# One decoder layer step on one core: decode softmax steps one key group later, small loads on three queues, a weight split forward

## The chip, the cores and the metric

The kernel runs on one core of one Trainium2 chip. The metric is the device time of one execution in microseconds (us). The kernel before takes 1120.18 us (median of three runs, 1119.37 to 1123.1).

## The reference

One step of a hybrid layer over 512 prompt tokens and 8 single decode tokens, all in float32. After an adaptive RMS norm a projection `w_in` feeds two groups of heads: a gated linear recurrence (RG-LRU) and latent attention (MLA). Cut to what matters here:

```python
mod = silu(c) @ w_ada + b_ada                      # shift, scale and gate of both halves
z = (rms_norm(x, norm1_g) * (1 + scale1) + shift1) @ w_in
x_lru, g_lru, q_lat, kv_lat, k_rope = split(z)
lru_out = rg_lru(causal_dwconv(x_lru)) * gelu(g_lru)
q = rms_norm(q_lat, q_lora_norm_g) @ w_uq;  kv_lat = rms_norm(kv_lat, kv_lora_norm_g)
# decode, for each of 8 sequences: 4096 cached keys (paged) and the new one, 8 heads
lat = concat(cache_lat[pages], lat_new)            # 4097 x 128
kv = lat @ w_ukv;  k_nope = rms_norm(kv[..., :64], k_nope_g);  v = kv[..., 64:]
p = softmax((q_nope . k_nope + q_rope . kr) * 96 ** -0.5);  attn = p @ v
x = x + gate1 * (concat(norm(lru_out), norm(attn)) @ w_o)
x = x + gate2 * gated_conv_mlp(...)                # w_up, w_down: the largest products
```

## The kernel before

Every engine has a program of its own, written by hand in the order in which it runs; semaphores join them. TensorE (PE) uses four PSUM tiles `ps0` to `ps3` in a fixed rotation: each piece of work has a job number j and takes `ps[j % 4]`, so PE may start job j only when job j - 4 has been read out by ScalarE (ACT) or VectorE (DVE) (`claim`).

**Start.** SyncE (SP) issues the inputs and the 24 chunks of `w_ada` of 1 MB into a ring of four slots; chunks 4 and on wait until PE has used the slot (`chunk_used`). ACT first issues 25 small loads (parameter rows, decode states, the page table), then a tanh (L1329) which the first product needs. PE turns x (eight jobs), does chunks 0 and 1, turns the parameter rows, does chunks 2 and 3.

**Input projection.** Twelve column tiles of `w_in`, `w0` to `w11`, are each split by ACT into a high part (`in_high`) and by GpSimd (POOL) into a low part (`in_low`), and PE multiplies them (`w_in(n)`, 48 matmuls each). `IN_ORDER` is the order of PE's jobs. ACT's `gate_branch(k)` reads out the gate tiles: `gate_branch(0)` frees the PSUM tile of `w8`. `nq`, `nkv`, `kr0` are sums of squares for three norms; ACT's `rstd` turns each into a reciprocal root.

**Decode.** Each of the 8 sequences is a unit v of 33 key tiles in nine groups g (eight of four tiles, one of one). PE runs two groups ahead with transposes: at group g it turns the latents of group g + 2 (at g = 7 and 8 those of groups 0 and 1 of the next unit), then multiplies group g (L1174). ACT copies the turned latents (L1512) and their high part (L1513), POOL takes the low part (`low_latents`, L795), and PE's group g waits for that. ACT squares the keys (L1528), DVE sums them (L2009).
The softmax of unit v - 1 lies within unit v: DVE `scores_max` in group 1 (L1964 to L1971), POOL `all_max` at g = 2 (L779, a maximum over all partitions), DVE `shift` in group 2 (L1976), ACT `probs` (L1506), DVE `prob_sums` (L1981), and PE `pv` (L1130, L1134) after group `PV_AT` = 4. When `pv` is done, the latents of unit v - 1 may be overwritten, and POOL fetches those of unit v + 1 into their place with two indirect DMAs of 1 MB (`cached_latents`, L749); the first half is needed by the transposes of group 0 of the next unit, at g = 7. POOL runs all this in one fixed order. In POOL's program the compiler puts an instruction MODIFY_POOL_CONFIG ahead of the maximum (before its wait), and another behind it.

Of the kernel before, what the change touches and what calls it, by code (L numbers as in the profile page):

```python
# [32 lines left out]
P = 128  # L33
# [78 lines left out]
class Steps:  # L112
# [20 lines left out]
    def leave(self, laps):  # L133
# [18 lines left out]
            + ["w6", "r4", "w7", "c3", "w8", "w9", "nq", "nkv", "kr0", "r5", "w10", "c4", "w11", "kr1", "c5"])  # L152
# [55 lines left out]
PV_AT = 4  # L208
# [49 lines left out]
def build(nc, t):  # L258
    with ExitStack() as ctx:
# [308 lines left out]
        def _(sp):  # L568
# [148 lines left out]
        def _(pool):  # L717
            nc.gpsimd.memset(par_rows[:, :, :], 0.0).then_inc(s_parz, 1)
            nc.gpsimd.memset(BD[:, :, :, :], 0.0).then_inc(s_bdz, 1)

# [78 lines left out]
            for v in range(1, NS + 1):  # L799
                for g in range(NG):  # L800
# [31 lines left out]
        def _(pe):  # L832
# [135 lines left out]
            w_in(9)  # L968
# [8 lines left out]
            both(j, C("blk", QK, R)[:, NOPE:QK], sq[NOPE:QK, 3, :], True, True, R).then_inc(psum_full[j % 4], 1)  # L977
            later_chunk(12)
# [309 lines left out]
        def _(act):  # L1288
# [19 lines left out]
            for name in ("b_ada", "norm1_g", "lru_conv_b", "lru_b_a", "lru_b_x", "lru_lambda",  # L1308
                         "q_lora_norm_g", "kv_lora_norm_g", "lru_out_norm_g", "mla_out_norm_g", "norm2_g"):
                load_rows(name, t[name].rearrange("l (r p) -> (l r) p", p=P))  # L1310

            load_rows("lru_conv_w", t["lru_conv_w"].rearrange("l w (r p) -> (l w r) p", p=P))
            for name, a, b in (("gq", "q_nope_norm_g", "q_rope_norm_g"), ("gk", "k_nope_norm_g", "k_rope_norm_g")):
                r = ROWS[name]
                act.dma_start(par_rows[r:r + 1, 0, 0:NOPE], t[a]).then_inc(s_par, 16)
                act.dma_start(par_rows[r:r + 1, 0, NOPE:QK], t[b]).then_inc(s_par, 16)
            fw = t["ffn_conv_w"].rearrange("l w (r p) -> (l w r) p", p=P)
            act.dma_start(par_rows[0:4 * FT, 1, :], fw[0:4 * FT, :]).then_inc(s_par, 16)
            act.dma_start(par_rows[0:2 * FT, 2, :], fw[4 * FT:6 * FT, :]).then_inc(s_par, 16)
            act.dma_start(par_rows[2 * FT:4 * FT, 2, :],  # L1320
                         t["ffn_conv_b"].rearrange("l (r p) -> (l r) p", p=P)).then_inc(s_par, 16)
            act.dma_start(st_tok, t["state_lru_conv"].rearrange("l b r w -> (l b r) w")).then_inc(s_par, 16)
            act.dma_start(h0_tok, t["state_lru_h"].rearrange("l b w -> (l b) w")).then_inc(s_par, 16)

            for r in range(4):
                act.dma_start(page_of[r:P:4, :], t["page_table"].rearrange("b n -> n b"), allow_slow_non_contiguous=True).then_inc(s_pt, 16)
# [55 lines left out]
            in_high(9)  # L1382

# [131 lines left out]
            def unit(base, lap, e, v):  # L1515

                for g in range(NG):
# [13 lines left out]
                    if base != J_DEC and g == 2:  # L1531
# [675 lines left out]
```

## Time and profile before

| | |
|---|---|
| median of three runs | 1120.18 us |
| profiled execution | 1124.76 us |
| its span (first to last instruction) | 1123.0 us |
| busy: PE, DVE, ACT, POOL | 1005.5, 671.2, 537.9, 196.8 us |
| mean granted clock of PE | 0.937 of 2.4 GHz |

The page lists engines' busy time; the views used below are the waits (which engine stood still for whom), the timelines (instructions in order of time, with the idle time before each), the chain of work that ended last, and tables by stretch of time. Decode lies between 308 and 645 us.

### The profile page before, as it was taken

Reading aid. Unit: us, or ns where it says so; the run is one execution under the profiler, and the core shown is the slowest. Engines: PE = TensorE matmul, PEld = TensorE weight load, DVE = VectorE, ACT = ScalarE, POOL = GpSimd, SP = SyncE. Lnnn points to the kernel's source line nnn. Section 1 sums busy time; section 2 is a strip of 40 time slices with the busy share of each in tenths; the row PEclk is TensorE's granted clock in tenths of the full one; section 3 lists DMA queues with packets and bytes.
Section 4 is the critical chain, followed back from the end, with each engine's and each line's share of the span. In section 5 each row is a group of like instructions: output and inputs, shape, how many; then the busy total and the mean of one; then the engine's idle time right before and its main releaser. Section 6 shows DMA issues by size and latency. Waiting matters only on the chain.

```text
span 1123.0 us, 21332 instructions
## 1 busy us (share of the span) xinstructions
PE 1005.5 (90%) x7916; PEld 904.9 (81%) x7916; DVE 671.2 (60%) x1553; ACT 537.9 (48%) x875; POOL 196.8 (18%) x202
## 2 busy tenths in 40 slices
PE   6699989999797977978978699799999999999997
PEld 4388755444496977977878689699999999999997
DVE  4591356656676657567557545667777777753212
ACT  3314736555487758658658443344444434322210
POOL 0233231000123422432432202211000010100000
PEclk9699987988899999899899879899999999999999
DMA  8975534000100211211201014222423233263202
GB/s 292 303 244 180 187 117 156 13 10 2 49 18 20 95 50 45 93 34 60 92 21 56 1 38 132 51 76 75 112 75 110 77 94 93 81 177 91 71 3 77
DMA packets 110527, 100.28 MB, mean 89 GB/s; under 512 B 10451, under 2 KB 99454, under 8 KB 108381
## 3 DMA queue, kind: packets, MB, share of 16 engines
q1 hardware_dynamic: 105478, 78.36, 23.5%
q0 software_dynamic: 3456, 20.97, 5.3%
q8 instruction: 36, 0.59, 0.2%
q10 hardware_dynamic: 1539, 0.22, 0.1%
q14 instruction: 18, 0.15, 0.0%
HBM read 96.80 MB, written 2.94 MB: 89 GB/s over the span
## 4 chain that ended last, share of the span: by engine, by line
PE 70%; DVE 9%; ACT 8%; issue 8%; POOL 2%; DMA 1%; ACTq 1%; DVEq 0%; POOLq 0%; SPq 0%
PE ps L841 46%; PE ps L1174 12%; PE ps L836 4%; PE ps L1078 2%; PE ps L866 2%; POOL latents_low L795 2%; DMA RW<-w_ada 1%; PE ps L1134 1%; DVE RB L2009 1%; ACT RB L1528 1%; DVE RB L1893 1%; ACT RB L1512 1%; PE ps L1169 1%; PE ps L1042 1%; PE ps L1059 1%
## 5 line engine op out<-in xcount | busy, mean ns | idle before, releaser
L841 PE MATMUL ps<-normed_high,up_weights_high 128*128 128x260 f32 x704 | 142.7, 284 | 3.6 <-DVE normed_low L1728 3.4
L841 PE MATMUL ps<-normed_high,up_weights_low 128*128 128x260 f32 x704 | 142.3, 284 | 0.0
L841 PE MATMUL ps<-normed_low,up_weights_high 128*128 128x260 f32 x704 | 142.1, 284 | 0.0
L795 POOL TENSOR_TENSOR latents_low<-RB,latents_high 128x512 fp32r<-128x512 f32 (+1 forms) x72 | 86.1, 1202 | 274.6 <-ACT latents_high L1513 224.6
L1174 PE MATMUL ps<-key_weights_high,latents_high 128*128 128x260 f32 x528 | 120.7, 312 | 13.0 <-DVE RB L2007 11.8
L841 PEld LDWEIGHTS ps<-normed_high,up_weights_high 128*128 128x128 f32 x704 | 109.2, 190 | 4.3 <-issue 3.5
L1174 PE MATMUL ps<-key_weights_low,latents_high 128*128 128x260 f32 x528 | 111.4, 294 | 0.0
L1575 ACT ACTIVATE up_weights_high<-RW 128x1024 fp32r<-128x1024 f32 x44 | 46.6, 1060 | 135.4 <-PE ps L841 132.9
L1174 PE MATMUL ps<-key_weights_high,latents_low 128*128 128x260 f32 x528 | 111.3, 294 | 0.0
L841 PEld LDWEIGHTS ps<-normed_high,up_weights_low 128*128 128x128 f32 x704 | 109.0, 189 | 0.0
L841 PEld LDWEIGHTS ps<-normed_low,up_weights_high 128*128 128x128 f32 x704 | 108.8, 189 | 0.0
L1174 PEld LDWEIGHTS ps<-key_weights_high,latents_high 128*128 128x128 f32 x528 | 87.2, 204 | 16.7 <-DVE RB L2007 14.7
L1174 PEld LDWEIGHTS ps<-key_weights_high,latents_low 128*128 128x128 f32 x528 | 86.8, 201 | 0.0
L1174 PEld LDWEIGHTS ps<-key_weights_low,latents_high 128*128 128x128 f32 x528 | 86.8, 201 | 0.0
L2088 DVE TENSOR_TENSOR up_weights_low<-RW,up_weights_high 128x1024 fp32r<-128x1024 f32 x44 | 54.9, 1251 | 34.3 <-ACT up_weights_high L1575 29.9
L1528 ACT ACTIVATE qrot<-ps 128x512 f32<-128x512 f32 x88 | 52.9, 601 | 45.4 <-PE ps L1174 41.7
L841 PE MATMUL ps<-hidden_high,down_weights_high 128*128 128x260 f32 x352 | 71.4, 284 | 1.3 <-issue 1.3
L2006 DVE COPY RB<-ps 128x32 f32<-128x32 f32 (+1 forms) x72 | 13.6, 188 | 96.1 <-ACT qrot L1528 52.4
L841 PE MATMUL ps<-hidden_high,down_weights_low 128*128 128x260 f32 x352 | 70.8, 282 | 0.0
L841 PE MATMUL ps<-hidden_low,down_weights_high 128*128 128x260 f32 x352 | 70.7, 282 | 0.0
L2077 DVE TENSOR_TENSOR d<-ps,modT 128x8 f32<-128x8 f32 x16 | 2.7, 166 | 107.8 <-PE ps L841 107.8
L828 POOL COPY UT<-RW 128x10 f32 x44 | 24.8, 563 | 238.9 <-ACT RW L1601 238.9
(282 smaller groups left out, 2268.4 us busy)
## 6 DMA issues: line engine op xcount, KB each, us to landing
RW<-w_ada SPq DMA_DIRECT2D x24, 1024.0 KB, 7.9
RW<-w_up SPq DMA_DIRECT2D x44, 512.0 KB, 5.0
RW<-w_down SPq DMA_DIRECT2D x8, 1408.0 KB, 7.1
RW<-w_in SPq DMA_DIRECT2D x11, 512.0 KB, 8.3
RB<-w_o SPq DMA_DIRECT2D x8, 512.0 KB, 4.7
RB<-x_prompt SPq DMA_DIRECT2D x2, 1024.0 KB, 7.1
o_y_p<-RB SPq DMA_DIRECT2D x4, 512.0 KB
wuq<-w_uq SPq DMA_DIRECT2D x8, 96.0 KB, 2.1
```

What stands on the lines that cost most here:

```text
L795: nc.gpsimd.tensor_tensor(latL[:, g % 3, c:4 * P], turned[:, g % 3, c:4 * P], latH[:, g % 3, c:4 * P].bitcast(F32), ALU.subtract).then_inc ...
L828: nc.gpsimd.tensor_copy(UT[:, bass.ds(FT * g + 2 * i + e, 1), :], UU[e][:, g, NP:UW]).then_inc(s_ut, 1)
L836: return nc.tensor.transpose(out, in_, ident[0:n, 0:n])
L841: last = mm(ps[j % 4][rows[0]:rows[1], h, 0:H], lhsT, src[:, h * H:(h + 1) * H], start=start, stop=stop)
L866: last = mm(flat(j)[32 * g:32 * g + 32, 0:256], cT[:, k, :], ring[:, q if n < 2 else q % 2, kk, 256 * g:256 * g + 256], start=(k == 0), st ...
L1042: last = mm(flat(J.vw[e])[:, VD * a:VD * a + VD], kvT[:, P * a:P * a + P], wukv[:, e, NOPE:P], start=True, stop=True)
L1078: last = mm(flat(J.pv[e])[VD * e:VD * e + VD, P * a:NP], hb[e]["v"][:, VD * a:VD * a + VD], hb[e]["pt"][:, a, P * a:NP], start=(a == 0), s ...
L1174: last = mm(ps[j % 4][:, h, 0:KWW], a[:, g % 3, at:at + P], b[:, e, h, :], start=(i == 0), stop=(i == 2))
L1528: A(sqd[c % 3].rearrange("p (h n) -> p h n", h=2), ps[j % 4][:, :, 0:4 * NOPE], ACT.Square).then_inc(s_sqd, 1)
L1575: A(wuH[:, KT * g:KT * g + KT, :], wup[:, c, KT * g:KT * g + KT, :], ACT.Copy).then_inc(s_whi, 1)
L2006: V.tensor_copy(srd[e][:, HEADS * c:HEADS * c + w], flat(j)[:, KWW:KWW + w]).then_inc(s_snc, 1)
L2088: V.tensor_tensor(wuL[:, KT * g:KT * g + KT, :], wup[:, c, KT * g:KT * g + KT, :], wuH[:, KT * g:KT * g + KT, :].bitcast(F32), SUB).then_i ...
```

## The change

Three things are edited. In decode, `PV_AT` is 5; POOL's `all_max` stands behind `low_latents(v, 4)` instead of ahead of it; ACT's `probs` stands after group 3, DVE's `shift` in group 3 and `prob_sums` after group 4. At the start, 15 of ACT's small loads are issued by SP behind its first four `w_ada` chunks, and the four of the page table by POOL. In the projection, ACT splits `w10` right behind `w9`; PE does `nq`, `nkv`, `kr0` ahead of `w9`; ACT's three `rstd` come ahead of `gate_branch(0)`, and DVE's use of them and two small steps (`mod_columns(3)`, `mod_rows(4)`) come earlier.

```diff
-            + ["w6", "r4", "w7", "c3", "w8", "w9", "nq", "nkv", "kr0", "r5", "w10", "c4", "w11", "kr1", "c5"])
+            + ["w6", "r4", "w7", "c3", "w8", "nq", "nkv", "kr0", "w9", "r5", "w10", "c4", "w11", "kr1", "c5"])
...
-PV_AT = 4
+PV_AT = 5
...  (SP)
-            for c in range(8):
-                if c >= 4:
-                    chunk_used(sp, c - 4)
+            for c in range(4):
+                modulation(c, c, s_ada[c])
+            sp.wait_ge(s_parz, 1)
...
+            for name in ("q_lora_norm_g", "kv_lora_norm_g", "lru_out_norm_g", "mla_out_norm_g", "norm2_g"):
+                load_rows(name, t[name].rearrange("l (r p) -> (l r) p", p=P))
...
+            sp.dma_start(h0_tok, t["state_lru_h"].rearrange("l b w -> (l b) w")).then_inc(s_par, 16)
+
+            for c in range(4, 8):
+                chunk_used(sp, c - 4)
...  (POOL)
+            for r in range(4):
+                nc.gpsimd.dma_start(page_of[r:P:4, :], t["page_table"].rearrange("b n -> n b"), allow_slow_non_contiguous=True).then_inc(s_pt, 16)
...
-                    if v > 1 and g == 2:
-                        all_max(v % 2, v - 1)
                     if g + 2 < NG:
                         low_latents(v, g + 2)
                     elif v < NS:
                         low_latents(v + 1, g + 2 - NG)
+                    if v > 1 and g == 2:
+                        all_max(v % 2, v - 1)
...  (PE)
-            w_in(9)
             norm_sum(J_NQ, 2, KT)
             norm_sum(J_NKV, 1, KT + 2, 2)
...
+            w_in(9)
             later_chunk(12)
...  (ACT)
             in_high(9)
+            in_high(10)
...
             nc.scalar.preload_act_table_set("natural_log_exp_and_others")
+            rstd(J_NQ, QL, dst=sq[:, 0, :]).then_inc(s_rs, 1)
+            rstd(J_NKV, KV, dst=sq[:, 1, :]).then_inc(s_rs, 1)
+            rstd(J_KR[0], 1, (NOPE, QK), dst=sq[NOPE:QK, 2, :]).then_inc(s_rs, 1)
             gate_branch(0)
-            in_high(10)
...
-                    if base != J_DEC and g == 2:
+                    if base != J_DEC and g == 3:
                         probs(1 - e, v - 1)
...  (DVE)
+            mod_columns(3)
+            mod_rows(4)
             dve.wait_ge(s_ta, 4)
...
-                        if base != J_DEC and (g, n) == (2, 1):
+                        if base != J_DEC and (g, n) == (3, 1):
                             shift(1 - e, v - 1)
                     if base != J_DEC:
-                        if g == 3:
+                        if g == 4:
                             prob_sums(1 - e, v - 1)
```

POOL, around the maximum in the first unit that has one; `latents_low` rows are groups 2 and on of the unit. Before:

```order
40 L795 TENSOR_TENSOR latents_low<-RB,latents_high 128x512 [waits psum_free2,latents_transposed_copied]
41 L795 TENSOR_TENSOR latents_low<-RB,latents_high 128x512 [waits psum_free3,latents_transposed_copied]
42 L779 ISA
43 L779 ISA RB<-RB 128x8 [waits partition_max_done]
44 L795 ISA
45 L795 TENSOR_TENSOR latents_low<-RB,latents_high 128x512 [waits psum_free0,latents_transposed_copied]
46 L795 TENSOR_TENSOR latents_low<-RB,latents_high 128x512 [waits psum_free1,latents_transposed_copied]
47 L795 TENSOR_TENSOR latents_low<-RB,latents_high 128x512 [waits psum_free2,latents_transposed_copied]
48 L749 DMA RW<-cache_kv_latent,half_of 128x2048 [waits psum_full3]
```

The same place in the changed kernel, whose lines are numbered 24 higher:

```order
41 L819 TENSOR_TENSOR latents_low<-RB,latents_high 128x512 [waits psum_free2,latents_transposed_copied]
42 L819 TENSOR_TENSOR latents_low<-RB,latents_high 128x512 [waits psum_free3,latents_transposed_copied]
43 L819 TENSOR_TENSOR latents_low<-RB,latents_high 128x512 [waits psum_free0,latents_transposed_copied]
44 L803 ISA
45 L803 ISA RB<-RB 128x8 [waits partition_max_done]
46 L819 ISA
47 L819 TENSOR_TENSOR latents_low<-RB,latents_high 128x512 [waits psum_free1,latents_transposed_copied]
48 L819 TENSOR_TENSOR latents_low<-RB,latents_high 128x512 [waits psum_free2,latents_transposed_copied]
49 L819 TENSOR_TENSOR latents_low<-RB,latents_high 128x512 [waits psum_free3,latents_transposed_copied]
50 L773 DMA RW<-cache_kv_latent,half_of 128x2048 [waits psum_full0]
```

Both MODIFY_POOL_CONFIG (the rows that say only ISA) and the maximum stand one low part later, and three low parts stand between them and the fetch as before, now those of groups 5, 6 and 7.

PE, from `pv` to the transposes that wait for the fetched latents. Before, the first rows after `pv` (transposes of group 7) and, after groups 5 and 6, the transposes of the next unit:

```order
839 L1134 MATMUL ps<-RW,RB 32x128 [waits psum_free3]
840 L1134 MATMUL ps<-RW,RB 32x128 x32
841 L836 MATMUL ps<-cst,RW 128x128 [waits psum_free1]
842 L836 MATMUL ps<-cst,RW 128x128 x4
...
861 L836 MATMUL ps<-cst,RW 128x128 [waits new_token_tile_done,psum_free2]
862 L836 MATMUL ps<-cst,RW 128x128
...
882 L836 MATMUL ps<-cst,RW 128x128 [waits cached_latents0_in0,cached_keys_in0]
883 L836 MATMUL ps<-cst,RW 128x128 x4
```

The changed kernel:

```order
859 L1158 MATMUL ps<-RW,RB 32x128 [waits psum_free0]
860 L1158 MATMUL ps<-RW,RB 32x128 x32
861 L860 MATMUL ps<-cst,RW 128x128 [waits new_token_tile_done,psum_free2]
862 L860 MATMUL ps<-cst,RW 128x128
...
882 L860 MATMUL ps<-cst,RW 128x128 [waits cached_latents0_in0,cached_keys_in0]
883 L860 MATMUL ps<-cst,RW 128x128 x4
```

The transposes of group 8 now follow `pv` directly: one group, not two, lies between `pv` and the row that waits for the fetch.

ACT, from the split of `w9` (the first row) to the read-out of `w8` (`gate_branch(0)`, L1393 before). Before:

```order
65 L1342 ACTIVATE input_weights_high<-RW 128x1024 [waits psum_full0,w_in_in0]
66 L1385 ACTIVATE RB<-RB,small 128x520 x4
67 L1388 ACTIVATE RB<-RB,small 128x520 [waits act_steps]
68 L1388 ACTIVATE RB<-RB,small 128x520 x3
69 L1395 ACT_TABLE_LOAD
70 L1393 ACTIVATE RB<-ps 128x520 [waits psum_full2]
71 L1342 ACTIVATE input_weights_high<-RW 128x1024 [waits psum_full2,w_in_in1]
```

The changed kernel, lines 7 or 8 higher (the `rstd` helper is L1321 and L1323):

```order
49 L1349 ACTIVATE input_weights_high<-RW 128x1024 [waits psum_full0,w_in_in0]
50 L1349 ACTIVATE input_weights_high<-RW 128x1024 [waits psum_full2,w_in_in1]
51 L1393 ACTIVATE RB<-RB,small 128x520 x4
52 L1396 ACTIVATE RB<-RB,small 128x520 [waits act_steps]
53 L1396 ACTIVATE RB<-RB,small 128x520 x3
54 L1403 ACT_TABLE_LOAD
55 L1321 ACTIVATE sq<-ps,small 128x520 [waits psum_full3]
56 L1323 ACTIVATE sq<-sq 128x520 [waits psum_free3]
57 L1321 ACTIVATE sq<-ps,small 128x520 [waits psum_full0]
58 L1323 ACTIVATE sq<-sq 128x520 [waits psum_free0]
59 L1321 ACTIVATE sq<-ps,small 32x520 [waits psum_full1]
61 L1401 ACTIVATE RB<-ps 128x520 [waits psum_full2]
```

The read-out of `w8` stands behind three `rstd`, and in `IN_ORDER` `w9` is now four jobs after `w8`, so PE's `w9` waits for this read-out.

## Rows read from the trace of the kernel before

**Rows 1.** Waits, decode (305:642): engine, line, for whom; us in total, times, longest.

```profile
POOL latents_low L795 <- issue: 50.0, 7, 7.6
PE ps L1169 <- POOL latents_low L795: 33.9, 7, 5.3
POOL RW L749 <- PE ps L1134: 32.5, 6, 6.1
```

**Rows 2.** Timeline of POOL, one unit: start us, us, engine, line, operation [idle before].

```profile
476.80 1.29 POOL L795 TENSOR_TENSOR latents_low<-RB,latents_high 128x512 fp32r<-128x512 f32 x1 [2.08 <-ACT latents_high L1513]
484.26 0.40 POOL L779 PARTITION_ALL_REDUCE RB<-RB  x1 [6.16 <-issue]
491.93 3.73 POOL L795 TENSOR_TENSOR latents_low<-RB,latents_high 128x512 fp32r<-128x512 f32 x3 [7.28 <-issue]
500.61 1.19 POOL L749 DMA_INDIRECT RW<-cache_kv_latent,half_of  x1 [4.95 <-PE ps L1134]
```

**Rows 3.** Chain of work, same unit (478:486), pieces in order: start us, us, what.

```profile
478.32 0.01 POOLq L779
...
480.50 3.76 issue
```

**Rows 4.** Timelines of DVE and POOL, the last maximum of the kernel.

```profile
643.22 0.62 DVE L1971 TENSOR_REDUCE RB<-RB 128x8 f32<-128x264 f32 x1
643.98 0.40 POOL L779 PARTITION_ALL_REDUCE RB<-RB  x1 [10.25 <-DVE RB L1971]
```

**Rows 5.** Timeline of ACT and PE, same unit as rows 2.

```profile
479.15 0.60 ACT L1513 ACTIVATE latents_high<-ps 128x512 fp32r<-128x512 f32 x1
487.53 0.73 PE L836 MATMUL ps<-cst,RW 128*128 128x128 f32 x5
493.24 0.64 PE L1169 MATMUL ps<-QBD,RB 128*128 x2 [4.97 <-POOL latents_low L795]
498.15 2.15 PE L1134 MATMUL ps<-RW,RB 128*32 128x128 f32 x66
503.92 0.38 PE L836 MATMUL ps<-cst,RW 128*128 128x128 f32 x2
507.23 0.71 PE L836 MATMUL ps<-cst,RW 128*128 128x128 f32 x5
```

**Rows 6.** The line L749, its issues at 458.4 and at 585.8 alone.

```profile
DMA to landing us min/median/max: 5.6/5.6/5.6
DMA to landing us min/median/max: 6.1/6.1/6.1
```

**Rows 7.** Table by stretch: from:to us, busy (count) by engine, PE clock, DMA share, GB/s.

```profile
20.00:24.00 4.00, 4.00 (x47) 2.07 (x49) 3.90 (x8) 1.91 (x3) 0.00 (x0) 1.00 0.46 112
493.20:496.40 3.20, 3.16 (x14) 3.17 (x15) 0.34 (x3) 0.60 (x1) 2.46 (x2) 0.50 0.00 0
```

**Rows 8.** Timelines of PE (two rows) and ACT in the input projection.

```profile
124.99 0.51 PE L841 MATMUL ps<-normed_high,input_weights_high 128*128 128x260 f32 x2 [0.74 <-DVE newrow L1664]
130.85 3.78 PE L841 MATMUL ps<-sq,cst 128*128 128x260 f32 x16
134.32 0.69 ACT L1297 ACTIVATE sq<-ps,small 128x520 f32<-128x520 f32 x1
137.68 0.63 ACT L1299 ACTIVATE sq<-sq 32x520 f32<-32x520 f32 x1
```

**Rows 9.** Timeline of PE in the prompt attention, two short waits.

```profile
176.05 1.04 PE L841 MATMUL ps<-RB,cst 96*32 96x260 f32 x4 [0.95 <-DVE RB L1862]
178.53 1.34 PE L841 MATMUL ps<-RB,cst 96*32 96x260 f32 x4 [1.44 <-DVE RB L1862]
```

**Rows 10.** Timelines of the start: ACT, PE and SP's queue.

```profile
12.27 1.28 ACT L1329 ACT_TABLE_LOAD   x1 [12.27 <-issue]
14.48 6.30 PE L836 MATMUL ps<-cst,RB 128*128 128x128 f32 x25 [2.50 <-DVE cT L1682]
22.51 0.37 SPq L583 DMA_DIRECT2D RW<-w_ada  x1
```

More of the change, by code:

```diff
@@ L597, in w_in, with load_rows @@
                 sp.dma_start(RA[:, n % 3, :, at:at + w], wi[:, :, P * m:P * m + w]).then_inc(s_win[n % 3], 16)
-            for c in range(8):
-                if c >= 4:
-                    chunk_used(sp, c - 4)
+            for c in range(4):
+                modulation(c, c, s_ada[c])
+            sp.wait_ge(s_parz, 1)
+            def load_rows(name, src):
+                n = src.shape[0]
+                sp.dma_start(par_rows[ROWS[name]:ROWS[name] + n, 0, 0:src.shape[1]], src).then_inc(s_par, 16)
+            for name in ("q_lora_norm_g", "kv_lora_norm_g", "lru_out_norm_g", "mla_out_norm_g", "norm2_g"):
+                load_rows(name, t[name].rearrange("l (r p) -> (l r) p", p=P))
+            load_rows("lru_conv_w", t["lru_conv_w"].rearrange("l w (r p) -> (l w r) p", p=P))
+            for name, a, b in (("gq", "q_nope_norm_g", "q_rope_norm_g"), ("gk", "k_nope_norm_g", "k_rope_norm_g")):
+                r = ROWS[name]
+                sp.dma_start(par_rows[r:r + 1, 0, 0:NOPE], t[a]).then_inc(s_par, 16)
+                sp.dma_start(par_rows[r:r + 1, 0, NOPE:QK], t[b]).then_inc(s_par, 16)
+            fw = t["ffn_conv_w"].rearrange("l w (r p) -> (l w r) p", p=P)
+            sp.dma_start(par_rows[0:4 * FT, 1, :], fw[0:4 * FT, :]).then_inc(s_par, 16)
+            sp.dma_start(par_rows[0:2 * FT, 2, :], fw[4 * FT:6 * FT, :]).then_inc(s_par, 16)
+            sp.dma_start(par_rows[2 * FT:4 * FT, 2, :],
+                         t["ffn_conv_b"].rearrange("l (r p) -> (l r) p", p=P)).then_inc(s_par, 16)
+            sp.dma_start(st_tok, t["state_lru_conv"].rearrange("l b r w -> (l b r) w")).then_inc(s_par, 16)
+            sp.dma_start(h0_tok, t["state_lru_h"].rearrange("l b w -> (l b) w")).then_inc(s_par, 16)
+            for c in range(4, 8):
+                chunk_used(sp, c - 4)
                 modulation(c, c % 4, s_ada[c % 4])
@@ L1306, in load_rows @@
                 act.dma_start(par_rows[ROWS[name]:ROWS[name] + n, part, 0:src.shape[1]], src).then_inc(s_par, 16)
-            for name in ("b_ada", "norm1_g", "lru_conv_b", "lru_b_a", "lru_b_x", "lru_lambda",
-                         "q_lora_norm_g", "kv_lora_norm_g", "lru_out_norm_g", "mla_out_norm_g", "norm2_g"):
+            for name in ("b_ada", "norm1_g", "lru_conv_b", "lru_b_a", "lru_b_x", "lru_lambda"):
                 load_rows(name, t[name].rearrange("l (r p) -> (l r) p", p=P))
[L1312 to L1326, printed above, removed]
             full(act, J_C)
@@ L1797, in _ @@
             v = st.did(V.scalar_tensor_tensor(TI[:, :, :], TI[:, :, :], 1.0, XC[:, :, :], ADD, MUL))
+            mod_columns(3)
+            mod_rows(4)
             dve.wait_ge(s_ta, 4)
             V.tensor_scalar(TA[:, :, :], TA[:, :, :], 1e-18, None, ALU.max).then_inc(s_tiny, 1)
-            mod_columns(3)
-            mod_rows(4)
+            dve.wait_ge(s_rs, 2)
+            for k in range(2):
+                V.scalar_tensor_tensor(qlT[:, k, :], qlT[:, k, :], pr("q_lora_norm_g", k), sq[:, 0, :], MUL, MUL).then_inc(s_ql, 1)
+            dve.wait_ge(s_rs, 3)
+            V.scalar_tensor_tensor(kvT[:, :], kvT[:, :], pr("kv_lora_norm_g"), sq[:, 1, :], MUL, MUL).then_inc(s_kvn, 1)
             dve.wait_ge(s_lru, 1)
@@ L1813, in _ @@
             dve.wait_ge(s_lrud, 1)
-            dve.wait_ge(s_rs, 2)
-            for k in range(2):
-                V.scalar_tensor_tensor(qlT[:, k, :], qlT[:, k, :], pr("q_lora_norm_g", k), sq[:, 0, :], MUL, MUL).then_inc(s_ql, 1)
-            dve.wait_ge(s_rs, 3)
-            V.scalar_tensor_tensor(kvT[:, :], kvT[:, :], pr("kv_lora_norm_g"), sq[:, 1, :], MUL, MUL).then_inc(s_kvn, 1)
             dve.wait_ge(s_rs, 4)
```

3 lines of the change are left out of this document (removed).

## The prediction

> **What bounds the kernel now.** I read the page first (PE is busy 90% of the span, so PE's waits are what an edit can win), then the waits of the decode stretch, then the timelines of one unit. Decode has one wait of size: PE's first key product of group 4 waits for the low part of its latents, seven times, 33.9 us in all, and POOL stood idle before that low part for 50.0 us with no releaser but its own issue [rows 1]. The timeline of POOL in one unit shows what it did: the low part of group 3 ends at 478.09, the maximum over partitions runs at 484.26 for 0.40 us, the next low part starts 7.28 us later, at 491.93 [rows 2]. ACT had delivered that low part's input at 479.75, PE had finished its transposes of the group at 488.3 and starts at 493.24 after 4.97 us of waiting [rows 5]. A maximum of 0.40 us thus holds POOL for 13.8 us. The chain splits the time ahead of the maximum: MODIFY_POOL_CONFIG is issued at 478.32, the row maxima arrive 2.15 us later, and from their arrival at 480.50 it takes 3.76 us more [rows 3]. From the config it is 5.94 us. In the last maximum of the kernel POOL had been idle for 10.25 us with its config long issued; the row maxima end at 643.84 and it starts at 643.98, 0.14 us later [rows 4]. So the time ahead runs from the config, not from the release, and a long wait hides it.
>
> The second thing to read is slack. `pv` ends at 500.30, POOL issues the fetch at 500.61 [rows 2, 5], its first half lands 5.6 to 6.1 us after issue [rows 6], so at about 506.4, and PE's transposes that need it run at 507.23 [rows 5]. That is 0.8 us of slack, all there is.
>
> **The change in decode, for the unit of rows 2.** The low part of group 4 now runs first: input at 479.75, a start 0.13 us later, 1.29 us long, so to 481.2, and the config is issued 0.2 us later at 481.4 instead of 478.32: 3.1 us later. By then the row maxima (480.5) are there and add nothing. The maximum runs at 481.4 + 5.94 = 487.3, and the next low part, now that of group 5, starts at 487.3 + 0.40 + 7.28 = 495.0 and lets PE go 1.3 us after that (as 491.93 to 493.24), at 496.3. PE gains on the way: group 4 needn't wait, DVE's `shift` no longer stops it for about a microsecond in group 3. But group 4 and the transposes of group 7 are done near 492, and PE then stands 4 to 5 us before group 5. The wait has moved by one group and kept its size. From the release, group 5 takes what group 4 took in the same place (493.24 to 497.94, the half-speed clock included: the stretch 493.20 to 496.40 has granted clock 0.50, that is the 1.2 GHz level [rows 7]), 4.7 us, and `pv` with the gap ahead of it 2.36: `pv` ends at 503.4 and the transposes of group 8 start at 503.3. Before they started at 503.92 [rows 5]. So the moved maximum is worth 0.6 us a unit.
>
> Then the fetch. It may start only when `pv` is done: 503.4 + 0.31, and lands 5.8 us later at 509.5. PE has one group left to do instead of two (3.31 us, 503.92 to 507.23 [rows 5]), is ready at 506.6 and stands for 2.9 us. The transposes run at 509.5 instead of 507.23: +2.3 us a unit (2.1 to 2.6 with the two landing times and a few tenths on POOL). PE had no wait there.
>
> The new wait also costs clock. After a wait of 1.44 us four matmuls took 1.34 us, after one of 0.95 us 1.04 [rows 9], so 0.3 lost; after 4.97 us the clock was 0.50 for 3.2 us [rows 7], so 1.6 lost. For 2.9 us I take 0.9 (ends 0 and 1.6), and assume that the clock has recovered from the first wait by then, as it had at 500. A unit: +3.2 us. Six units fetch [rows 1]: 19.2. The last unit has no fetch and keeps its 0.6: decode +18.6. ACT's and DVE's moved steps (`probs`, `prob_sums`) cost nothing: they end near 490, while PE stands till 496. If that cover went, `prob_sums` (0.6 us) would be late by less than itself.
>
> Here a page of the Trainium skill weighs in. GPSIMD Engine Reference, Instruction dispatch, says that the first call after newly loaded code pays about 6 us, measured from MODIFY_POOL_CONFIG less the wait for the event, so counted from the release. Rows 3 agree on the size only if the wait is left in, and rows 4 (0.14 us after a long wait) speak against counting from the release; what it would do here is the first rival.
>
> **The input projection.** Before, PE's `w9` started at 124.99 and the three sums at 130.85 for 3.78 us [rows 8]. Now the sums go first, from 124.8 (DVE frees their tile 0.2 us earlier) to 128.5. `w9` then needs the PSUM tile of `w8`, which ACT reads out only after three `rstd`. Those take from 134.32 to 138.31 in the trace, 4.0 us [rows 8]; the first waits for `nq`, half of the sums' 3.78 us, so 126.7, the third ends at 130.7, the read-out (0.6) at 131.3. PE stands for 2.8 us, and ends `w9` at 137.1 instead of ending the sums at 134.56: +2.6, and 0.8 for the clock by the same rule: +3.4 (2.4 to 4.4). The split of `w10` moved forward adds 1.0 us to ACT ahead of this, which is in ACT's shadow before 126.7; the LRU chain on ACT and DVE runs some 6 us later, but was ready 10 us before its reader at 154.6, so hidden. What follows moves with PE.
>
> **The start.** ACT issues DMAs until 12.27 and only then loads its table and does the tanh; PE stands 2.50 us for it at 14.48 [rows 10]. With six loads left ACT is free at 3.6, the tanh is done before x has landed, and PE runs on. The `w_ada` chunk that needs the first slot goes out at 20.0 instead of 22.51 [rows 10]; between 20 and 24 the DMA engines are only 0.46 busy [rows 7], and everything to the first `w_in` product is paced by them, so the 2.5 us carry through. Against it, the parameter rows now stand in SP's queue behind 4 MB and PE wants them at 20.9, where it reached them at 23.24; a wait of 3 us there costs little as the chunks already issued go on. -2.5 us (ends -3.3 and +0.5). The page table's four loads on POOL take a few us of its first 34 idle ones. The skill (DMA: Bandwidth & Descriptors, Issuing engines are not separate DMA queues) says that issuing from several engines saves only the sequencer's time; by it nothing lands sooner, and the gain is ACT's issue time alone, which no row of the other two queues contradicts.
>
> **Sum.** +18.6 + 3.4 - 2.5 = +19.5 us on the profiled execution (1124.76, span 1123.0), which stands 4.6 above the median of 1120.18; on that, 1139.7. I say 1139.
>
> **The rivals.**
> 1. *Counted from the release.* If the time ahead of the maximum ran from the release (3.76 us), the change would put it at 481.4 + 3.6 = 485.0, 2.3 us sooner than I say. PE's group 5 starts at 494.0, and if the shorter wait keeps the clock up it takes 3.1 us; `pv` ends at 499.5, the fetch lands at 505.6, the unit is 1.6 shorter, less 0.9 for clock: 6 x -0.7, the last unit -4.5, with the other two terms +0.9: 1112. For it: in seven units the time from the release hardly varies; against it: rows 4. This one ends faster. 6%.
> 2. *The fetch is in time*, since PE is late by other means or the fetch lands sooner. Then only -0.6 a unit is left: 7 x -0.6 + 0.9, 1117. Against it: the shortest landing is 5.6 us, PE's work in between 3.31. 6%.
> 3. *The new waits cost no clock*: 19.5 - 6 x 0.9 - 0.8 = +13.3, 1133; and at the other end 1.6 each gives 1145. This lies in the forecast's own range (1130 to 1148).
> 4. *The start gives nothing and the parameter rows are late:* +3 more, 1142; in the range too.
>
> **Chances.** Forecast (with 3 and 4) 85%, rival 1 6%, rival 2 6%, something else between them 3%. The range of 8 in 10 is 1126 to 1147. 0.3% is 3.4 us, what a measurement tells from no change. Faster: rival 1 and half of rival 2, 0.09; same 0.06; slower 0.85.
>
> **What would show it.** In the profile after: the maximum 5.9 us after a config issued 3 us later; PE's wait for a low part in group 5, not 4, of 4 to 5 us; a new wait of PE on the DMA of the cached latents, six times, 2.5 to 3 us, about 17 us in all; in the projection a wait of about 2.8 us for ACT's read-out ahead of `w9`; at the start no wait for the tanh and the first `w_in` product at about 44 instead of 46.4. Wrong it would be if the DMA wait is missing (then the landing was misread), if group 5 starts before 495 in that unit's time (rival 1), or if the clock after the new wait stays at 1.0.

## The result and the profile after

| | before | after |
|---|---|---|
| median of four runs | 1121.34 us | 1150.15 us |
| profiled execution, its span | 1124.76, 1123.0 us | 1151.27, 1149.4 us |
| mean granted clock | 0.937 | 0.930 |

The ratio is 1.0244, 95% interval 1.0209 to 1.0279: slower by 27 us (by the ratio) to 29 us (by the medians), where +19.5 (1139, range 1126 to 1147) was forecast from 1120.18, the median of three of the four runs before. The measured time lies above the range. The direction and the main mechanism were right, the size was not.

Lines of the changed kernel are 24 higher on POOL and PE and 7 or 8 higher on ACT and DVE. The waits of its decode stretch (310:670), which answer to [rows 1]:

```profile
PE ps L1193 <- POOL latents_low L819: 34.1, 7, 5.4
PE ps L860 <- DMA RW<-cache_kv_latent,half_of: 16.2, 6, 2.8
PE ps L1198 <- DVE RB L2014: 8.1, 8, 1.1
POOL latents_low L819 <- issue: 49.8, 7, 7.6
POOL RB L803 <- issue: 41.7, 7, 6.1
POOL RW L773 <- PE ps L1158: 35.0, 6, 6.4
```

The first row kept its size (33.9 before), though it now stands ahead of group 5. The second is new. POOL in one unit, against [rows 2] (the same unit, the fourth with a maximum; its times are later because what lies ahead of it has grown):

```profile
498.44 1.28 POOL L819 TENSOR_TENSOR latents_low<-RB,latents_high 128x512 fp32r<-128x512 f32 x1 [1.80 <-ACT latents_high L1520]
505.69 0.40 POOL L803 PARTITION_ALL_REDUCE RB<-RB  x1 [5.97 <-issue]
513.24 3.73 POOL L819 TENSOR_TENSOR latents_low<-RB,latents_high 128x512 fp32r<-128x512 f32 x3 [7.15 <-issue]
523.37 1.19 POOL L773 DMA_INDIRECT RW<-cache_kv_latent,half_of  x1 [6.41 <-PE ps L1158]
```

The maximum comes 5.97 us after the low part ahead of it, although the row maxima had been there before its config was issued: DVE's last step on them (L1978) ends at 498.98, MODIFY_POOL_CONFIG is issued at 499.94, and the maximum starts 5.75 us after that. In the seven units with such a wait it starts 5.6 to 5.9 us after the config in both kernels, though the row maxima come 2.1 to 2.4 us behind the config before and 0.7 to 1.0 us ahead of it after. So the 6 us run from the config, as the prediction read it. PE in the same unit, against [rows 5]:

```profile
508.96 0.73 PE L860 MATMUL ps<-cst,RW 128*128 128x128 f32 x5
514.62 0.63 PE L1193 MATMUL ps<-QBD,RB 128*128 x2 [4.93 <-POOL latents_low L819]
520.77 2.30 PE L1158 MATMUL ps<-RW,RB 128*32 128x128 f32 x66
523.00 0.44 PE L860 MATMUL ps<-cst,RW 128*128 128x128 f32 x2
529.25 0.74 PE L860 MATMUL ps<-cst,RW 128*128 128x128 f32 x5 [2.69 <-DMA RW<-cache_kv_latent,half_of]
```

The wait before the last row is the fetch landing late. Three stretches of this kernel, in the columns of [rows 7] (the last three are clock, DMA share, GB/s), show what the waits do to the clock: group 5 behind its 4.93 us wait, the groups behind the DMA wait of 2.69 us just shown, and the group behind an earlier DMA wait of 2.55 us.

```profile
514.60:520.40 5.80, 5.78 (x26) 5.79 (x27) 1.98 (x7) 1.79 (x3) 2.36 (x2) 0.50 0.00 0
529.00:534.50 5.50, 5.25 (x45) 5.28 (x46) 2.76 (x9) 4.22 (x8) 1.31 (x1) 1.00 0.35 144
482.00:487.30 5.30, 5.24 (x32) 5.27 (x33) 1.81 (x7) 2.88 (x5) 1.28 (x1) 0.68 0.38 155
```

Group 5 of this unit runs wholly at the 1.2 GHz level and takes 5.8 us; group 4 took 4.7 in the same place before [rows 5]. That pair is not typical, though. The group behind the long wait takes 4.7 to 5.8 us from unit to unit in both kernels, 5.26 on average before and 5.42 after. Behind the DMA wait the clock falls in some units and not in others: the group there takes 5.2 us in four of the six, and 3.7 in two. The input projection, against [rows 8], ACT and PE:

```profile
115.45 1.06 ACT L1349 ACTIVATE input_weights_high<-RW 128x1024 fp32r<-128x1024 f32 x1
122.84 1.06 ACT L1349 ACTIVATE input_weights_high<-RW 128x1024 fp32r<-128x1024 f32 x1 [6.33 <-PE ps L865]
123.80 2.94 ACT L1393 ACTIVATE RB<-RB,small 128x520 f32<-128x520 f32 x4
131.04 0.69 ACT L1321 ACTIVATE sq<-ps,small 128x520 f32<-128x520 f32 x1
135.05 0.60 ACT L1401 ACTIVATE RB<-ps 128x520 f32<-128x520 f32 x1
```

```profile
124.36 3.89 PE L865 MATMUL ps<-sq,cst 128*128 128x260 f32 x16 [0.62 <-DVE newrow L1671]
135.71 0.80 PE L865 MATMUL ps<-normed_high,input_weights_high 128*128 128x260 f32 x2 [7.46 <-ACT RB L1401]
159.64 1.06 PE L865 MATMUL ps<-krT,cst 32*32 32x260 f32 x4 [0.62 <-DVE newrow L1671]
```

PE stood 7.46 us before `w9`, not 2.8. ACT's second row tells why: it stood 6.33 us for PE, at the split of `w10`. The start, against [rows 10], PE and DVE:

```profile
8.09 10.05 PE L860 MATMUL ps<-cst,RB 128*128 128x128 f32 x40 [2.69 <-DMA RB<-x_prompt]
25.43 0.71 PE L860 MATMUL ps<-cst,par_rows 109*128 109x109 f32 x3 [4.82 <-DMA RB<-state_lru_h]
42.04 0.66 PE L860 MATMUL ps<-cst,newrow 128*128 128x128 f32 x2 [2.06 <-DVE newrow L1671]
45.67 0.77 PE L865 MATMUL ps<-normed_high,input_weights_high 128*128 128x260 f32 x2 [2.96 <-DVE input_low L1735]
```

```profile
32.22 9.20 DVE L1714 TENSOR_TENSOR RB<-xT,rs 128x512 f32<-128x512 f32 x8 [0.17 <-ACT rs L1323]
```

The tanh no longer holds PE, but the last small load does, and `w_in` starts at 45.67 (46.41 before).

**Where the 26.4 us of span went.** To the first `w_in` product -0.7, of which 0.5 is left at PE's last chunk ahead of the sums (122.67, before 123.18). From there to `kr1` +9.0 (37.0 us, before 28.0). Prompt attention, from `kr1` to the first key product, -1.0. Decode +21.3: the key products L1174 run from 310.9 to 639.1 before, 328.2 us, and after

```profile
L1198 PE MATMUL ps<-key_weights_high,latents_low x528: 277/283/420, 318.3 to 667.8; 128*128 128x260 f32 x176
```

349.5 us (columns: ns min/median/max, first and last start). From the last `pv` to the end -2.3 (476.4 and 474.1 us), in code that is the same. I call the 328.2 the *decode length* below; it is the measure that tells kernels apart best, since it leaves out the prompt attention, whose length varies (last section). The four other kernels below whose decode is that of before (e2, e3, e6, e7) have 328.2 to 328.8. The parts outside decode are less sure: from the last `pv` to the end the same code varies by 4.8 us over all the profiles, so the -2.3 says nothing of the change.

### The profile page after: what moved, and what is told of

Its sections match the earlier page's. It is cut to its first block, busy times and chain, and to the rows that moved or that the text cites. A ratio compares the mean times of both kernels' runs of the same rounds, so it can differ in the third digit from the quotient of the medians.

```text
span 1149.4 us, 21320 instructions
## 1 busy us (share of the span) xinstructions
PE 1011.2 (88%) x7916; PEld 911.3 (79%) x7916; DVE 677.2 (59%) x1553; ACT 539.1 (47%) x875; POOL 198.6 (17%) x206
## 4 chain that ended last, share of the span: by engine, by line
PE 66%; DVE 11%; ACT 9%; issue 6%; DMA 5%; POOL 1%; SPq 1%; DVEq 0%; ACTq 0%; POOLq 0%
PE ps L865 44%; PE ps L1198 12%; DMA RW<-cache_kv_latent,half_of 3%; PE ps L860 3%; PE ps L1102 2%; PE ps L890 2%; PE ps L1158 1%; DVE RB L1900 1%; DVE RB L2016 1%; ACT qrot L1535 1%; ACT RB L1519 1%; DMA RB<-state_lru_h 1%; ACT latents_high L1520 1%; DVE RB L1714 1%; PE ps L1193 1%
## 5 line engine op out<-in xcount | busy, mean ns | idle before, releaser
L1198 PE MATMUL ps<-key_weights_high,latents_high 128*128 128x260 f32 x528 | 123.5, 318 | 9.7 <-DVE RB L2014 8.1
L1198 PE MATMUL ps<-key_weights_low,latents_high 128*128 128x260 f32 x528 | 114.5, 301 | 0.0
L1198 PEld LDWEIGHTS ps<-key_weights_high,latents_high 128*128 128x128 f32 x528 | 89.8, 210 | 13.1 <-DVE RB L2014 11.0
L1198 PEld LDWEIGHTS ps<-key_weights_low,latents_high 128*128 128x128 f32 x528 | 90.0, 208 | 0.0
L1198 PEld LDWEIGHTS ps<-key_weights_high,latents_low 128*128 128x128 f32 x528 | 89.5, 207 | 0.0
L1535 ACT ACTIVATE krT<-ps 128x512 f32<-128x512 f32 x88 | 53.1, 604 | 48.3 <-PE ps L1198 46.0
L860 PE MATMUL ps<-cst,RW 128*128 128x128 f32 x336 | 50.2, 279 | 20.9 <-DMA RW<-cache_kv_latent,half_of 16.2
```

The costliest lines, as they stand in the source:

```text
L860: return nc.tensor.transpose(out, in_, ident[0:n, 0:n])
L1198: last = mm(ps[j % 4][:, h, 0:KWW], a[:, g % 3, at:at + P], b[:, e, h, :], start=(i == 0), stop=(i == 2))
L1535: A(sqd[c % 3].rearrange("p (h n) -> p h n", h=2), ps[j % 4][:, :, 0:4 * NOPE], ACT.Square).then_inc(s_sqd, 1)
```

## The experiments

Each was run with the kernel before on the same chip; a ratio stands with its 95% interval.

**One part at a time.** `e1_decode_only`: the kernel before with

```diff
-PV_AT = 4
+PV_AT = 5
...  all_max behind low_latents(v, 4); probs after group 3, shift in group 3
...
-                        if g == 3:
+                        if g == 4:
                             prob_sums(1 - e, v - 1)
```

> The kernel before with the five edits of decode alone (PV_AT = 5, the maximum behind the low part of group 4, probs, shift and prob_sums one group on). Theory: decode carries most of the loss, 21 us of the 26.4 that the span grew (from the first decode stage to the last pv the trace after is 21.2 us longer), +21 (+19 to +23), with a wait of PE for the cached latents six times, 16 us in all, and the wait for the low part unchanged at 34. Rival A: part of that is a consequence of the late start of decode and of the clock it brings with it: alone the edits cost what the prediction said, +18.6 or less. Rival B: the parts do not add, decode alone costs under +15.

Measured: 1143.12 us against 1121.79, ratio 1.0178 (1.0138 to 1.0218), decode length 349.5, the same as in the full change. Waits of PE in its decode:

```profile
PE ps L1169 <- POOL latents_low L795: 34.6, 7, 5.4
PE ps L836 <- DMA RW<-cache_kv_latent,half_of: 16.9, 6, 3.0
```

The theory holds: decode costs +21.3 by the trace, in company or alone. Rival B is out. Rival A's figure (+18.6) is inside the interval of the times; it is the decode length, the same to a tenth in both kernels, that speaks against it.

`e2_projection_only`: the kernel before with the projection's edits, `in_high(10)` behind `in_high(9)` among them.

> The kernel before with the edits of the input projection alone (w10's split behind w9's, the sums and ACT's three rstd ahead of w9 and gate_branch(0), DVE's steps moved). Theory: PE waits 7.5 us for the read-out of w8, +8 (+7 to +9.5) in time. Rival: the wait is swallowed later, where PE waits for ACT and DVE in the prompt attention, and the time grows by +3.4 or less, as the prediction said.

Measured: 1132.7 us, ratio 1.0100 (1.0070 to 1.0131), +11.2. PE and ACT:

```profile
134.69 0.80 PE L841 MATMUL ps<-normed_high,input_weights_high 128*128 128x260 f32 x2 [7.46 <-ACT RB L1394]
```

```profile
121.82 1.06 ACT L1342 ACTIVATE input_weights_high<-RW 128x1024 fp32r<-128x1024 f32 x1 [5.46 <-PE ps L841]
```

The same 7.46 us, and nothing later swallows them. By the times this is more than the +7 to +9.5 expected, but their interval (+7.9 to +14.7) reaches into it; from the last chunk ahead of the sums to `kr1` the trace gives 37.2 us against 28.0, +9.2. `e3_projection_no_split` keeps the split in its old place:

```diff
             in_high(9)
-            in_high(10)
...
             gate_branch(0)
+            in_high(10)
```

> As the last one, but the split of w10 stays behind gate_branch(0). Theory: it is the split's wait for PE's end of w8 (at 122.8) ahead of ACT's eight exps and tanhs that made ACT 5 us late; without it ACT does these from about 119 on, the first rstd starts when the sum nq is there, PE waits 2.8 us for the read-out of w8 as the prediction had it, +3.4 (+2 to +4.5). w10 itself may then wait a little for its own split, up to 1 us. Rival: ACT is late for another reason (the three rstd with their table, the order of nq, nkv, kr0), and the wait stays above 6 us, +7 or more.

Measured: 1128.44 us, ratio 1.0060 (1.0017 to 1.0104). PE:

```profile
129.98 0.51 PE L841 MATMUL ps<-normed_high,input_weights_high 128*128 128x260 f32 x2 [2.84 <-ACT RB L1393]
```

2.84 us, to the tenth what the prediction gave for the order of the sums and `rstd`. From the last chunk ahead of the sums to `kr1` it takes 31.0 us (121.57 to 152.58), against 28.0 before (28.7 and 28.4 in e4 and e13, which have the same order) and 37.2 in e2: the sums ahead of `w9` cost some 3 us, the split alone 6.2. The times agree, but their interval is too wide to tell e3 from e2 by itself (1128.44 against 1132.7); it is the trace that does.

**Which edit of decode.** `e5_pv_late`: the maximum, `shift` and `probs` stay, only `PV_AT = 5` and `prob_sums` after group 4.

> The kernel before with PV_AT = 5 and prob_sums after group 4 alone; the maximum, shift and probs stay where they were. Theory: the loss of decode comes from pv, not from the maximum. pv ends one group (3.3 us) later, the fetch goes out and lands later by as much, one group only is left to cover it: PE waits about 3.3 - 0.8 = 2.5 to 3.2 us for the cached latents, six times (15 to 19 us), and the wait for the low part of group 4 keeps its 34 us. With the clock that is +19 to +26 us, take +22. Rival: it is the maximum's new place that makes the fetch late (its low parts of groups 5 to 7 are queued ahead of the fetch on POOL), then PV_AT alone costs under +10.

Measured: 1146.58 us, ratio 1.0257 (1.0210 to 1.0304), decode length 355.8. Its waits:

```profile
PE ps L1169 <- POOL latents_low L795: 32.8, 7, 5.0
PE ps L836 <- DMA RW<-cache_kv_latent,half_of: 17.4, 6, 3.1
```

`PV_AT` (with its sum) alone makes the loss, and a bigger one than with the maximum moved: the later maximum is worth 6.3 us of decode length to its credit. `e4_maximum_late` is the other half: everything of decode but `pv` and its sum.

```diff
 PV_AT = 4
...  all_max behind low_latents(v, 4); probs after group 3, shift in group 3
                         if g == 3:
                             prob_sums(1 - e, v - 1)
```

> The kernel before with the maximum behind the low part of group 4, probs after group 3 and shift in group 3, but PV_AT = 4 and prob_sums after group 3. Theory: pv then runs while POOL still reloads, in PE's wait ahead of group 5: group 4 ends near 492 in the time of the prediction's unit, pv near 494.5, PE waits some 2 us for the low part and starts group 5 at 496.3 instead of 500.3, the fetch is issued near 498 instead of 500.6 and lands ahead of its reader (two groups lie between). A unit is 2.5 to 4 us shorter, seven units: -17 to -28, take -20. Rival: probs and prob_sums come too late for pv at group 4 (the maximum's result is there near 487.7, then shift, exp and sum), pv and with it group 5 start as late as before or later, 0 to +10.

Measured: 1088.66 us, ratio 0.9720 (0.9654 to 0.9786). A second time, as `e13_maximum_late_again`:

> The late maximum with PV_AT = 4 once more, on the chip of the two runs around it, to compare them with. Theory: 1089 (1086 to 1092), 0.970 to 0.974 of the kernel before. Rival: the first figure of this kernel rests on a fast prompt attention (its granted clock was 0.90 there, 0.83 in the kernel before), which it doesn't keep: then 1096.

Measured: 1093.36 us (six runs), ratio 0.9717 (0.9678 to 0.9756). The kernel is some 32 us faster than before, more than the -17 to -28 expected of e4. The second time lies between the theory (1086 to 1092) and its rival (1096), the ratio inside the theory's; and the rival is right in one thing: the first profile had a fast prompt attention (below). Decode length 299.5 and 299.7. PE around the maximum in e4, and its waits:

```profile
470.26 0.39 PE L1130 MATMUL ps<-RB,cst 128*128 128x8 f32 x2 [0.47 <-DVE RB L2007]
470.57 2.15 PE L1134 MATMUL ps<-RW,RB 128*32 128x128 f32 x66
472.66 0.77 PE L836 MATMUL ps<-cst,RW 128*128 128x128 f32 x5
474.99 0.41 PE L1169 MATMUL ps<-QBD,RB 128*128 x2 [1.56 <-POOL latents_low L795]
```

```profile
PE ps L1169 <- POOL latents_low L795: 9.7, 6, 1.9
PE ps L836 <- DMA RW<-cache_kv_latent,half_of: 2.4, 4, 0.7
```

`pv` (2.15 us, with its sum 2.36) and group 4 now lie in the time that POOL is away, and 1.56 us of wait are left of 4.97. Of the 28.7 us of decode length, 24.2 are this wait (33.9 to 9.7). PE's busy time over decode fell from 242.0 to 233.7 with the clock up from 0.93 to 0.98, which is 8.3 more; the rest are smaller waits of both signs, 2.4 us for the DMA (second row), 3.3 us of `pv` for its sum and 2.2 us once for ACT on the one side, 3.8 less for DVE on the other. The estimate of -20 lacked the clock. The rows of both kernels over decode:

```profile
352.00:640.00 288.00, 241.98 (x2197) 233.74 (x2196) 182.61 (x571) 193.38 (x359) 92.21 (x94) 0.93 0.15 53
```

```profile
344.00:604.00 260.00, 233.69 (x2197) 224.24 (x2197) 182.91 (x576) 194.09 (x359) 91.70 (x94) 0.98 0.17 59
```

**What the late fetch costs.** `e9_decode_no_fetch`, the kernel of e1 with

```diff
-                        cached_latents(v % 2, v)
...
-                    pe.wait_ge(s_lat[0][e], 8 * (v + 1 - e))
+                    pe.wait_ge(s_lat[0][e], 16)
```

> The five edits of decode, but POOL doesn't fetch the cached latents of units 3 to 8 (the first two stay in place), which leaves that part of the computation out. It shows what the fetch's lateness costs. Theory: without it the wait for the DMA (16.9 us in six) goes, and so does the clock that it costs, by the trace about 1.6 us each (a group after it took 5.2 us and not 3.65), 26 us together: the time falls to that of the kernel before less 7 x 0.6, 1117 (1113 to 1121). Rival A: the DMA's wait costs its length alone or 0.9 us of clock, as the prediction said: 1143 - 17 - 6 = 1120 or more, up to 1126. Rival B: PE only stands longer for the low part in its place (POOL's chain of config, maximum and reload sets the pace): no change against the kernel with the five edits, near 1143.

Measured: 1117.18 us, ratio 0.9965 (0.9942 to 0.9988), decode length 323.0. This kernel leaves out the fetches of six of the eight sequences. The DMA wait is gone, the wait for the low part is 34.2 us. Against e1 the decode length falls by 26.5 us, of which 16.9 are waits. The other 9.6, 1.6 for each of six waits, is the clock: PE's busy time over the decode length falls from 289.2 to 279.8 us, its granted clock rises from 0.91 to 0.94. And with its fetch left out the decode is 5.2 us shorter than before (328.2 to 323.0), close to the 7 x 0.6 = 4.2 of the prediction for the moved maximum; the kernel before without its fetch was not run. Rival B is out. Rival A is out by the decode length; the times by themselves (-24 us against e1, give or take 5) don't tell its 23 us from the theory's 26.

**The change, two numbers set back.** `e11_change_pv_back`, from the changed kernel:

```diff
-PV_AT = 5
+PV_AT = 4
...
-                        if g == 4:
+                        if g == 3:
                             prob_sums(1 - e, v - 1)
```

> The changed kernel with two numbers set back: PV_AT = 4 and prob_sums after group 3; all else (the later maximum, the start, the projection) as changed. Theory: the loss in decode is pv's place alone, so this gets all of the -33 us that the later maximum gave on the kernel before, less the projection's +11: 1098 (1093 to 1105). Rival: the gain of the later maximum depends on the rest of the timing, and with the projection's and the start's edits in, it is under 15 us against the kernel before.

Measured: 1101.03 us, ratio 0.9820 (0.9775 to 0.9865), decode length 299.2. These two numbers are worth 50 us of decode length, and turn a change that costs 2.4% into one that gains 1.8%.

**The start.** `e6_start_only`, the start's edits alone:

> The kernel before with the edits of the start alone. Theory: the gain of an earlier tanh (2.5 us) is given back by PE's wait of 4.8 us for the last small load, which stands behind 4 MB in SP's queue, and by DVE's eight steps L1714 (9.2 us and not 4.9) that now run beside POOL's splits. The first product of w_in starts 0.7 us sooner, time -0.7 (-2 to +1), no change that can be told. Rival: -2.5, the prediction's.

Measured: 1122.32 us (ten runs), ratio 0.9998 (0.9976 to 1.0021). The first product of `w_in` starts at 46.33, DVE's eight steps take 9.21 us. The interval still holds the rival's -2.5; it is the trace that speaks against it. `e7_start_act_after_tanh`, the fifteen loads on ACT behind the tanh:

```diff
             A(gmod[:, :, :].rearrange("p k n -> p (k n)"), flat(J_C)[:, 0:72], ACT.Tanh, scale=0.5).then_inc(s_silu, 1)
+            for name in ("q_lora_norm_g", "kv_lora_norm_g", "lru_out_norm_g", "mla_out_norm_g", "norm2_g"):
+                load_rows(name, t[name].rearrange("l (r p) -> (l r) p", p=P))
...
```

> The page table on POOL and six small loads ahead of ACT's tanh, as the change has it, but the other fifteen follow on ACT behind the tanh instead of on SP behind the chunks. Theory: PE runs through to the parameter rows without a wait, DVE's eight steps end before POOL starts its splits, and the first product of w_in starts at about 44: -2.5 us (-3.5 to -1). Rival: the chunks of w_ada set the pace (PE waited 4.2 us for one at 37.7 before), they are not sooner, and it is 0.

Measured: 1120.87 us (ten runs), ratio 1.0003 (0.9977 to 1.0028). Its PE and DVE:

```profile
20.88 0.47 PE L838 MATMUL ps<-cst,par_rows 109*128 109x109 f32 x3
35.73 1.94 PE L868 MATMUL ps<-RW,cT 128*32 128x256 f32 x16 [4.96 <-DMA RW<-w_ada]
44.48 0.77 PE L843 MATMUL ps<-normed_high,input_weights_high 128*128 128x260 f32 x2 [2.96 <-DVE input_low L1727]
```

```profile
27.30 4.91 DVE L1706 TENSOR_TENSOR RB<-xT,rs 128x512 f32<-128x512 f32 x8 [0.16 <-ACT rs L1301]
```

Here PE has no wait at the parameter rows, DVE's steps take 4.91 us, and `w_in` starts at 44.48, near the 44 forecast; PE waits for the chunks instead (4.96 us). In the nine profiles with the old start (before, e1 to e5, e9, e12, e13) the first product of `w_in` starts between 45.06 and 47.73, in the three with the change's start (after, e6, e11) between 45.67 and 46.54, in the two with this one (e7, e10) at 44.48 and 44.77. So the change's start can't be told from the old one, and this one is ahead by 1 to 2 us in the trace, but not in the time. The intervals show that either start gives under 3 us; the exact worth is open, and so is the rival, by which the chunks set the pace.

**Towards the best.** `e12_fetch_early`, the kernel of e4 with the fetch ahead of the low part of group 6:

```diff
-                    if 1 < v < NS and g == PV_AT:
+                    if 1 < v < NS and g == PV_AT - 1:
                         full(pool, J_UNIT1 + UNIT * (v - 2) + UJ["pv", 0])
```

> The late maximum with PV_AT = 4, and POOL issues the fetch ahead of the low part of group 6 instead of behind it. Theory: pv is done 2.3 us before POOL issues anything, so the fetch goes out 1.3 us sooner and the waits of PE for the cached latents (2.4 us in four) go; the low part of group 6 comes 2.3 us later, its reader has 1 to 2 us of slack. -2.5 against the late maximum alone (-4 to 0), hard to tell. Rival: the low part of group 6 is now late for PE by 1 us or more in each of six units, +5 or more.

Measured: 1094.21 us, ratio 0.9734 (0.9702 to 0.9767), decode length 300.3. The DMA waits are gone, but

```profile
PE ps L1169 <- POOL latents_low L795: 13.4, 10, 2.4
```

ten waits instead of six (10.7 us in e13): what the fetch gained, the low part of group 6 gave back. A miss: the rival is right in kind, not in size. `e10_best` has that and the start of e7:

> All that helped: the late maximum with PV_AT = 4, the earlier fetch, and the start with the fifteen small loads on ACT behind the tanh. Theory: the parts add, 1089 - 2.5 - 1 = 1085.5 (1081 to 1090). Rival: the start's part moves nothing (its own run gave 1.0003 with 0.25% of uncertainty), and the fetch's nothing or the wrong way: 1089 or more.

Measured: 1091.3 us, ratio 0.9710 (0.9672 to 0.9748), decode length 299.4. It beats both kernels, by some 32 us the one before and by 59 us the changed one (1150.15, run at another time), but isn't told apart from e4 alone, which is the simpler one. The forecast 1085.5 (1081 to 1090) was not reached; the rival is right that the two additions move nothing that can be measured.

## Why the prediction was wrong, step by step

1. *The time of the maximum runs from its config, and moving it keeps the wait.* Right: 5.97 us with the release long there, PE's wait 34.1 us in seven, in group 5.
2. *The moved maximum is worth 0.6 us a unit.* Nearly right: 5.2 us in seven (e9), 6.3 between e5 and e1, where 4.2 were forecast.
3. *The fetch lands late, 2.9 us in each of six units.* Right: 16.2 us, 2.7 each. e9 shows that the fetch is the cause of the wait, e5 and e11 that it is `PV_AT` that makes the fetch late.
4. *Clock, 0.9 us for each new wait.* Too small. The bounds 0 and 1.6 were on record, the value taken lay between; e9 gives 1.6 a wait, the upper end. In the change PE's busy time over the decode length grew by 8.2 us (281.8 to 290.0) where six times 0.9 is 5.4, and decode came to +21.3 instead of +18.6. Of the 2.8 us between the two, 0.9 lie behind the new wait itself (1.5 to 1.6 us more in four units of six and nothing in two, 6.3 in all). Another 1.1 lie in the group behind the long wait, which the prediction took as unchanged; the rest is spread over PE's other work. The unit of [rows 5], from which the 4.7 us were read, has the shortest such group of the seven (5.26 on average); this error stands on both sides of the difference and drops out.
5. *The split of `w10` moved forward is in ACT's shadow before 126.7.* This is the step that failed most, and the term that was mis-sized most: I counted the split's 1.0 us of work and put its wait at nothing. The split also waits, `[waits psum_full2,w_in_in1]` in its row of ACT's order: it may overwrite its buffer only when PE has done with `w8`, at 122.8. Before the change eight exps and tanhs (5.9 us) and a table load (1.3 us) stood ahead of that wait and filled it; now they stand behind it. ACT lost 6.33 us, PE got `w8`'s tile back 4.4 us later than forecast (135.7, not 131.3), and the clock took 1.5 us more (48 matmuls of `w9` in 7.3 us, 5.9 before). The projection came to +9.0 instead of +3.4; e3 gives 3.0 with this one row put back.
6. *The start: -2.5, a late parameter row costs little.* Wrong in size: -0.7. The last small load was issued at 14.70 and landed 10.6 us later, PE stood 4.82 us for it, more than the 2.50 us for the tanh that were saved. It then pushed DVE's eight steps beside POOL's first splits, where they took 9.20 us instead of 4.91, and DVE was late for the last chunk by 2.06 us (`[2.06 <-DVE newrow L1671]`). "The chunks already issued go on" was true, and the time was lost all the same, since norm, steps and splits come behind the rows.

The profile's row for the late load, in SP's queue, is

```profile
14.70 0.58 SPq L620 DMA_DIRECT2D RB<-state_lru_h  x1
```

against 11.18 on ACT's queue in e7, where PE found it landed at 20.88. The semaphore of the small loads tells more: its last count comes at 25.30 in the changed kernel and at 19.21 in e7 (16.78 before, where the load was issued at 9.2). Of the 6.1 us between the first two, 3.5 are the later issue; the other 2.6 are a longer way, 10.6 us from issue to landing against at most 8.0 in e7 and 7.6 before. The fourth `w_ada` chunk, issued ahead of the load in both, landed at 22.75 in the changed kernel, ahead of the load in its own queue, and at 23.68 in e7, behind the load in the other queue. The Trainium skill bears on this (DMA: Bandwidth & Descriptors, Queues, rings and completion order): each DMA engine consumes the descriptors of one queue in order, and between queues it takes turns. I had used the neighbouring rule, that issuing from several engines saves only the sequencer's time, by which the choice of the queue would not matter. These landings agree with the first; the second alone doesn't give the 2.6 us.

The sum by these steps: 21.3 + 9.0 - 0.7 = 29.6, and -3.2 in code that didn't change. With step 5 alone put right the forecast would have been 1145; with steps 4 and 6 as well, 1149, next to the measured 1150. The prediction also names two ranges, 1126 to 1147 for the whole and, under its third rival, 1130 to 1148; the measured time lies above both.

## What to carry to other kernels

A step moved forward on an in-order engine carries its wait with it: before costing its work, read what it waits for, when that comes, and what used to stand in front of the wait. A long pause of one engine is best used, not moved: put the work that needs nothing of it (here `pv`) into the pause of the one that waits, and keep the distance between the last reader of a buffer and the fetch into it. Where a step that frees a buffer is tied to a fetch with 0.8 us of slack, a shift of 3 us of it can cost more than its length: in e5 six shifts of a 3.3 us group cost 27.6 us of decode length, for the clock falls with the wait.

## What the runs showed of the hardware

**Waits cost clock beyond their length, and not each time.** Six waits of 2.8 us cost 1.6 us each in e9's comparison, but the same length in e3 cost 0.1 us (48 matmuls of `w9` in 5.96 us, 5.86 before). Behind a DMA wait in decode the group took 5.2 us in four of the six units of the change and of e1 and in all six of e5, and 3.7 us in the others. In decode the engine had waited 4.9 us shortly before (until 514.62, the next wait begins at 526.6). That this is the reason is a reading and wasn't tried, and neither is it known why the clock fell behind one of the two DMA waits shown above (0.68) and not behind the other (1.00).

**The prompt attention has more than one length**, with the same instructions in the same order. From `kr1` to the first decode product it took 158.7 us before and 151.9 in e4, 162.5 in e13. The stretch 180:300 of e4 and of e13, which are one kernel:

```profile
180.00:300.00 120.00, 104.88 (x422) 58.45 (x422) 84.37 (x236) 63.63 (x142) 2.97 (x2) 0.90 0.07 16
```

```profile
180.00:300.00 120.00, 108.79 (x392) 58.46 (x390) 78.06 (x220) 60.30 (x137) 0.00 (x0) 0.82 0.04 10
```

The granted clock is 0.90 in one and 0.82 in the other. Between these two profiles, 8.2 us apart at their end, the time from `kr1` to the first decode product makes 10.6 us. That it is also why the times of a kernel spread over 10 us is likely but not shown, as the other executions have no profile. One profile must not be read by its end.

**DVE and POOL slow each other.** Eight DVE steps with two inputs took 9.20 us beside two of POOL's splits (5.25 us) and 4.91 alone (the splits 4.66, e7). The loss lies in two of the eight:

```profile
L1714 DVE TENSOR_TENSOR RB<-xT,rs x8: 678/682/2832, 32.2 to 40.7; 128x512 f32<-128x512 f32 x8
```

The third and the fourth step took 2.83 us each, the other six 0.68 to 0.69. Each of the two had started while one of the splits was running and ended 0.54 us after that split (35.72 and 36.26, 38.47 and 39.02). The Trainium skill (SBUF — State Buffer, Who interferes with whom) says that a DVE instruction with two inputs in SBUF contends with a GpSimd instruction that reads it, that the shared ports are locked and not divided, and that the order of issue decides who blocks; these rows agree.
